# Clearing the semaphores of closed stages together instead of at the end of each stage

## The reference, cut to what matters

```
def reference(...):
    x = first_block(x, c, positions, ...)     # HGRN2 + windowed attention, pool mixer, conv FFN
    return second_block(x, c_2, ctx_2, ...)   # mLSTM + attention, GLA, PEER experts

# the shape of a layer, second block
x = _layernorm(ALPHA * x + g1 * mixer(x * (1 + sc1) + sh1), ...)
f = _peer(x * (1 + sc2) + sh2, wq, keys, u, v)   # 128 experts of 16384 gathered per token
x = _layernorm(ALPHA * x + g2 * f, ...)
```

## Time and profile before

| what | us |
| --- | --- |
| median of three runs | 4278.11 |
| the three runs | 4261.40, 4278.11, 4279.54 |
| the profiled execution | 4276.59 |
| its span, first to last instruction | 4274.8 |
| TensorE busy | 3166.1 (74%) |
| VectorE busy | 2299.4 (54%) |
| ScalarE busy | 1045.3 (24%) |
| GpSimd busy | 932.1 (22%) |

### The profile page before, as it was taken

How to read it: one execution, slowest core, us unless ns; L and a number is a source line. 1 busy time by engine, 2 the same in 40 slices (tenths; PEclk the granted TensorE clock), 3 DMA queues, 4 the chain that set the end, 5 groups by cost and what they waited for, 6 DMA issues and landing times. The chain is left out here.

```text
span 4274.8 us, 37661 instructions
## 1 busy us (share of the span) xinstructions
PE 3166.1 (74%) x12012; PEld 1860.5 (44%) x12012; DVE 2299.4 (54%) x4802; ACT 1045.3 (24%) x2385; POOL 932.1 (22%) x804
## 2 busy tenths in 40 slices
PE   5767975977976868798777777777666664777776
PEld 1657933962734746233232232222264563322322
DVE  4456645746156338744665665555433648655554
ACT  1335422531232332111111111111232241111112
POOL 0000000000000012344444444444100023444442
PEclk9868997998986589999999999999987777999999
DMA  7214552536200111999999999999530034999996
GB/s 286 91 40 138 175 223 99 184 131 230 78 0 0 40 54 64 383 415 422 421 421 421 421 422 421 422 421 422 222 130 0 1 114 172 422 421 421 422 421 260
DMA packets 166466, 1052.95 MB, mean 246 GB/s; under 512 B 18332, under 2 KB 22172, under 8 KB 55344
## 3 DMA queue, kind: packets, MB, share of 16 engines
q0 software_dynamic: 110592, 805.36, 45.4%
q1 hardware_dynamic: 55728, 245.89, 16.0%
HBM read 1050.12 MB, written 1.05 MB: 246 GB/s over the span
## 5 line engine op out<-in xcount | busy, mean ns | idle before, releaser
L1800 PE MATMUL peer_fetch_summed<-peer_fetch_raw,peer_fetch_diag 128*128 128x512 f32 x3072 | 1443.4, 616 | 501.7 <-ACT peer_fetch_diag L1739 501.7
L1696 DVE CUSTOM_DVE_ANT_0 peer_fetch_raw<-peer_fetch_raw,peer_rows 128x1024 f32<-128x1024 f32 x768 | 940.2, 1225 | 852.6 <-DMA peer_fetch_raw<-in_peer_uv,peer_fetch_experts 852.1
L1800 PEld LDWEIGHTS peer_fetch_summed<-peer_fetch_raw,peer_fetch_diag 128*128 128x128 f32 x3072 | 567.2, 193 | 1368.7 <-ACT peer_fetch_diag L1739 777.4
L1618 POOL DMA_INDIRECT peer_fetch_raw<-in_peer_uv,peer_fetch_experts x768 | 855.6, 1114 | 1188.8 <-PE peer_fetch_summed L1800 1058.2
L1543 POOL TENSOR_TENSOR peer_keys_lo<-peer_pick_wq_raw,peer_keys_hi 128x1024 fp32r<-128x1024 f32 x32 | 76.3, 2389 | 2096.8 <-ACT peer_keys_hi L1502 2096.8
L1730 ACT ACTIVATE peer_fetch_gelu<-peer_fetch_score 128x2 f32<-128x2 f32 x384 | 78.1, 203 | 1629.2 <-DVE peer_fetch_score L1696 1629.2
L1739 ACT ACTIVATE peer_fetch_diag<-all_constants,peer_fetch_gelu 128x128 f32<-128x128 f32 x768 | 260.1, 386 | 0.5 <-issue 0.2
L124 PE MATMUL ffn_up_acc<-first_h_hi,ffn_up_hi 128*128 128x256 f32 x704 | 201.3, 286 | 36.9 <-DVE ffn_up_lo L644 36.9
L124 PE MATMUL ffn_up_acc<-first_h_lo,ffn_up_hi 128*128 128x256 f32 x704 | 200.9, 285 | 0.0
L124 PE MATMUL ffn_up_acc<-first_h_hi,ffn_up_lo 128*128 128x256 f32 x704 | 200.8, 285 | 0.0
L452 PE MATMUL mod_acc<-mod_weights,mod_act_c 128*1 128x512 f32 (+1 forms) x288 | 135.6, 615 | 43.9 <-DMA mod_weights<-in_ada_w 30.6
(11 more groups left out here) (483 smaller groups left out, 4808.0 us busy)
## 6 DMA issues: line engine op xcount, KB each, us to landing
mod_weights<-in_ada_w SPq DMA_DIRECT2D x48, 1024.0 KB, 7.4
in_up_raw<-in_w_up SPq DMA_DIRECT2D x88, 512.0 KB, 4.1
mod_weights<-in_w_mod SPq DMA_DIRECT2D x24, 1024.0 KB, 5.9
peer_fetch_next_raw<-in_w_mod SPq DMA_DIRECT2D x24, 1024.0 KB, 8.8
ffn_down_raw<-in_w_down SPq DMA_DIRECT2D x32, 704.0 KB, 5.6
peer_pick_wq_raw<-in_peer_wq SPq DMA_DIRECT2D x32, 512.0 KB, 3.3
peer_fetch_raw<-in_peer_uv,peer_fetch_experts POOLq DMA_INDIRECT x768, 19.0
in_in_raw<-in_ab_w_in SPq DMA_DIRECT2D x17, 512.0 KB, 3.4
```

Source lines behind the costliest of these rows:

```text
L1618: nc.gpsimd.indirect_dma_start(raw[:, n % ring].rearrange("p c d -> p (c d)"), None, uv_rows, bass.IndirectOffsetOnAxis(index[:, i, e:e + ...
L1696: nc.vector.tensor_tensor_reduce(raw[:, n % ring, 0, :], raw[:, n % ring, 0, :], rows[:, i, :], 1.0, 0.0, ALU.mult, ALU.add, score[:, i, e ...
L1800: ins = nc.tensor.matmul(summed[:, i % 2, half, :], diag[:, n % dring, :], raw[:, n % ring, 1, half * 512:(half + 1) * 512], start=(e == 0 ...
```

## The change

`__exit__` no longer clears and meets each time. A closed stage's semaphores go on a list common to all stages; when it holds more than 80, or when the outermost stage closes, GpSimd clears them all, the engines meet, and the list is emptied. Buffers are given back as before. Until they are cleared, the numbers aren't given out again.

```diff
+SPENT = 80
 class Stage:
+    spent = []
+
+    def __init__(self, nc, name, outermost=False):
+        self.nc, self.name, self.ctx, self.sems, self.outermost = nc, name, ExitStack(), [], outermost
 
     def __exit__(self, *_):
-        self.nc.clear_and_free_semaphores(self.sems)
-        self.nc.all_engine_barrier()
+        Stage.spent += self.sems
+        if len(Stage.spent) > SPENT or self.outermost:
+            self.nc.clear_and_free_semaphores(Stage.spent)
+            self.nc.all_engine_barrier()
+            Stage.spent = []
         self.ctx.close()
 
 def program(nc, d, out):
-    with Stage(nc, "all") as st:
+    with Stage(nc, "all", outermost=True) as st:
```

More of the change, by code:

```diff
@@ L35 @@
 ROUND = 12582912.0
+SPENT = 80
 class Stage:
-    def __init__(self, nc, name):
-        self.nc, self.name, self.ctx, self.sems = nc, name, ExitStack(), []
+    spent = []
+    def __init__(self, nc, name, outermost=False):
+        self.nc, self.name, self.ctx, self.sems, self.outermost = nc, name, ExitStack(), [], outermost
     def __enter__(self):
```

## The result

| | before | changed |
| --- | --- | --- |
| median, us | 4274.17 (6 runs) | 4232.62 (6 runs) |
| ratio | | 0.9912, 95% interval 0.9892 to 0.9932 |
| the profiled execution | 4276.59 | 4231.81 |
| its span | 4274.8 | 4230.0 |
| second meetings | 91 | 6 |

The change makes the kernel 0.9% faster: 38 us by the ratio, 29 to 46 by its interval, where 31 were forecast. The two profiled executions are 44.8 us apart. A stage's end is again the distance between the release of the last meeting before it and its own; these distances add up to 38.9 us before and 6.85 us after, so 32.0 us are the ends themselves. The other 12.8 us were gained inside the blocks, between the meetings, where no instruction was changed. Outside the two gathering stages the span shrank by 44 us, where less than 20 was to be the sign of a wrong prediction.

What follows compares the result with a forecast made beforehand. Transfers bound the two gathering stages, a serial chain of short stages the other 2210 us. 36.3 - 3.5 (joint clears) - 0.8 (late chunks) - 0.8 (code) = 31.2 us off, forecast 4246 us, range 4229 to 4263.

Steps and rivals of the forecast that it cites:

- the sign of a wrong prediction: Outside the gathering stages: the prediction is wrong if these 2210 us shrink by less than 20.
- The bound and the ends: Some 60 short stages in line, 2210 us: pauses between them are on the path; 91 ends sum to 38.9 us.
- Six meetings stay: At stage ends: 6 keep a clear and a meeting, 85 lose both; 36.3 us removed.
- The joint clears' price: At the six remaining ends: 428 semaphores in 11 ranges, 6.1 us in place of 2.6, so 3.5 us dearer.
- What is late next: Stages with chunks loaded ahead: third chunk of `ab_out` waits about 1.0 us instead of 0.6, `gla_out` likewise; 0.8 us taken back.
- one of the prediction's signs of being wrong: In the chunked stages: the prediction is wrong if a stage's granted clock has fallen.
- Code: Instruction streams: some 330 instructions fewer on GpSimd, 170 on each other engine; five dear ends; 0.8 us taken back.
- The clock: TensorE's stages: each clock return 3 us later costs 1.5 us, about twenty returns; a swing of 5 us either way likely.
- More than the sum: Shorter pauses: the clock falls less often, 10 us per 20 us low stretch avoided, about 4236 or 4225; chance 0.05.
- The sum's own best end: Whole kernel: all terms at their best bounds take 35.5 us off, 4243 us.
- an argument against a longer low level: Long chunked stages: the clock came back each time, and pauses now get shorter; put against the slower case.
- The slower rival: TensorE's stages, such as `ffn0_up`: the clock falls differently, against the change, making the kernel slower; chance 0.03.

Runs made afterwards that it cites:

- meet_twice: The kernel before with the second meeting of all engines written twice at each of the 91 ends; median 4302.6 us, 1.0050 of the kernel before.
- meet_always: The changed kernel, clears joined, but with the second meeting kept at all 91 ends; median 4271.7 us, 0.9985 of the kernel before.
- after_shift2: The changed kernel with two more meetings of all engines just before `window_attention`; median 4223.5 us, 0.9869 of the kernel before.

## Why the prediction was right or wrong

**The bound and the ends: right.** The short stages stand in line and their ends are on the path; `meet_twice` shows it from the other side: 91 further meetings lengthen the ends by 32.1 us and the time by 16 to 27.

**Six meetings stay: right. The joint clears' price: nearly.** 6.1 us were forecast for the six ends, 6.85 measured. 15 ranges were cleared and not 11: I had misjudged which numbers are given out again, and the outermost end takes 1.02 us for nine semaphores in five ranges, or (1.02 - 0.33) / 5 = 0.14 for a range. The price per semaphore (7.5 ns) came out at 7.0. Ends in all: 36.3 - 3.5 = 32.8 forecast, 32.0 measured.

**What is late next: right in place, too small.** The third chunk waits 0.86 us longer in `ab_out`, not 0.4, and in `gla_out` 0.46, with 0.40 at the second. `ab_out` took 28.6 us instead of 28.0, `gla_out` 0.1 to 0.3 less; the 0.8 us taken back can't be told from the clock's part in these stages. The clock of `ab_out` went from 0.90 (0.89 in the second profile) to 0.88 in both profiles of the changed kernel, which by the letter is one of the prediction's signs of being wrong; it costs half a microsecond, and the stages of 100 us and more with chunks kept theirs to 0.005.

**Code.** One end of the changed kernel's six stands out as five did before: that of `gla_qg` takes 1.57 us in both profiles. GpSimd starts its third clear 0.33 us after the drain ahead of it, and the same end in `meet_always` takes 1.27. So 0.3 us of the 0.8 taken back is seen, and it is also 0.3 of the 0.75 by which the joint ends were dearer. The rest would sit in the blocks and can't be separated there. This 0.8 us, half of the 1.6 by which five ends stood out before, was an estimate of mine; no run shows that term, nor what those ends wait for. What the runs show in its place is these 0.3 us.

**The clock: the term that was mis-sized.** In the sum it was nought, with a swing of 5 us either way, and the case "More than the sum", in which the clock falls less often, had a chance of 0.05. Over all executions the changed kernel's mean is 42 us under that of before (4275.9 to 4233.5), of which the ends are 32.0; the rest fell by 10.4 us. The scatter of the pooled executions (8.5 us before, 6.0 changed) gives that a standard error of about 2; the two chips by themselves give 3 and 14 us, with errors of 5 and 4, so its size is uncertain. The span at the low level fell by 55 us.

Laid against the clock's record, the two profiles of each kernel say where. The low level (0.50) lasts 868 and 884 us before, 825 in both changed; that is 51 us less on average. The ends hold 22 of them. TensorE's matmuls ran for 455 and 471 us at the low level before and for 433 and 438 changed, 27 us less, which at twice the speed (222 ns a matmul at the low level, 114 at the upper) is worth 13; the blocks are 13.3 us shorter on average. 7.2 of these are `window_attention`, whose cause stays open. The eight norms are worth 2.9 in these profiles: `ln00`, `ln01` and `ln30` gained 4.9 through the pause ahead of them and `ln10` 1.2, while `ln11` and `ln31`, which now have a joint end ahead, became longer by 1.7 and 1.3. The 5.3 us above are the mean over kernels some of which have no joint end there. The other 3 us are small steps in many stages.

So the direction was forecast, and the time lies in the range, 4232.6 in 4229 to 4263, but near its lower end. The sum's own best end was 4243; the time is in the range by the 14 us that were allowed below it for the clock and the scatter of the executions before, and not by the sum. I had named the pauses as what the clock falls in, and then not looked at what stands right behind each: the layer norms begin with 16 matmuls behind a pause, and their length of 18 us before, against the 16.5 of `ln11`, stood in the trace. The prediction counted the shorter pauses as an argument against a longer low level. `ln00`, `ln01` and `ln30`, 4.9 us shorter together, bear that out. `ln11` is a case against it: its pause went from 2.54 to 2.38 us, and it became 1.7 us longer. `window_attention` is another: its clock is at 0.50 with TensorE busy for 112.4 of 114.8 us (`after_shift2`).

**The slower rival** didn't come: `ffn0_up` stayed at 134.3 us and 0.97. At the low level's 222 ns a matmul in place of 114, its 1056 matmuls would have made it up to 114 us longer.

## What to carry to other kernels
A meeting of all engines behind another meeting cost 0.33 to 0.35 us between the releases each time in a kernel of short stages, the clear ahead of it on GpSimd only some 0.1 more; count them, and price one from its line. Where the clears can wait, they can run while no engine waits for GpSimd, and the numbers be given back after a meeting that is needed anyway; here that took the ends from 6.85 to 0.4 us, but no gain in time could be told. Where TensorE's first matmuls stand just behind such pauses, look at the granted clock in those stretches, since 1.30 us of pause in place of 2.0 to 2.5 was worth 1.7 us there, and a joint clear in such a place keeps the pause long (2.38 us ahead of `ln11`); and don't credit a shift of 7 us in one profile to the edit before a second profile and several executions have shown it.

## What was not expected of the hardware
With exactly the same instructions and no transfers, one stage of 400 matmuls took 103.2, 107.6 or 114.8 us, at granted clocks of 0.60, 0.56 and 0.50, and repeated its value in a second execution of the same kernel in all three kernels that were profiled twice. Two executions of one kernel can thus agree to 0.1 us in most stages, and still be 20 us apart from a third: those of the kernel before lay between 4250 and 4288.
